# Later head sums and two multiplications on GpSimd in a decoder step, with the hand-overs between its stages rearranged

## The reference, cut to what matters

```python
u = rmsnorm(x, norm_mix) @ w_in               # q/k/v, r/k/v + low ranks, two gates of 1024 columns
us = u + mu_rw * (u_prev - u)                  # token shift
r, k, v, wl, al, gl = split(us)
decay = exp(-exp(-softplus(-(w0 + tanh(wl) @ w2)) - 0.5))
a = sigmoid(a0 + al @ a2);  g = sigmoid(gl) @ g2
kk = heads(k * k_k) / norm_of_head(k * k_k)    # a sum over each head's 64 features
k_mod = k * (1 + (a - 1) * k_a)
S, o = scan(S * d - (S kk)(kk * a)^T + v k^T)  # over tokens
bonus = sum_of_head(r * k_mod * r_k) * v       # the second sum over each head: "head sums"
mixed = (sig(gA) * (oa @ p_a) + sig(gB) * ((norm(o) + bonus) * g @ p_b)) @ w_o
```

## Time and profile before

| | |
|---|---|
| median of 3 runs | 1637.89 us |
| profiled execution: its own time | 1645.24 us |
| its span | 1643.5 us |
| PE busy | 1514.0 us (92%) |
| DVE busy | 680.5 us (41%) |
| POOL (GpSimd) busy | 497.4 us (30%) |
| ACT busy | 362.0 us (22%) |
| mean granted TensorE clock | 0.970 |

### The profile page before, as it was taken

How to read it: one execution, slowest core, us unless ns; L and a number is a source line. 1 busy time by engine, 2 the same in 40 slices (tenths; PEclk the granted TensorE clock), 3 DMA queues, 4 the chain that set the end, 5 groups by cost and what they waited for, 6 DMA issues and landing times. The chain is left out here.

```text
span 1643.5 us, 29192 instructions
## 1 busy us (share of the span) xinstructions
PE 1514.0 (92%) x12025; PEld 869.6 (53%) x12025; DVE 680.5 (41%) x1295; ACT 362.0 (22%) x711; POOL 497.4 (30%) x506
## 2 busy tenths in 40 slices
PE   7999998989999999999999999899999599999992
PEld 4664455455777787755667775444444233323320
DVE  4203144433268887651554333235384222222225
ACT  3002144454123332011211111112012111111122
POOL 3001055654323345415334320000227312222224
PEclk9999999999999999989999999899999799999996
DMA  6603298999531112454231214654401779999997
GB/s 232 231 35 115 80 325 321 374 354 347 173 134 59 58 66 82 114 153 112 71 71 49 60 43 159 238 218 141 192 39 52 288 275 412 402 397 398 403 335 248
DMA packets 111478, 322.88 MB, mean 196 GB/s; under 512 B 31576, under 2 KB 41240, under 8 KB 100688
## 3 DMA queue, kind: packets, MB, share of 16 engines
q1 hardware_dynamic: 83200, 246.45, 40.7%
q0 software_dynamic: 26848, 70.25, 13.1%
q10 hardware_dynamic: 1296, 4.29, 0.7%
HBM read 270.78 MB, written 58.02 MB: 200 GB/s over the span
## 5 line engine op out<-in xcount | busy, mean ns | idle before, releaser
L1718 PE MATMUL gate_p<-rows,gate_w 128*128 128x352 f32 x576 | 182.5, 473 | 0.0
L1718 PEld LDWEIGHTS gate_p<-rows,gate_w 128*128 128x128 f32 x576 | 109.7, 194 | 63.9 <-ACT u_rw L1868 5.1
L2616 PE MATMUL x_p<-wgu,rows 128*32 128x512 f32 (+1 forms) x640 | 124.7, 616 | 2.8 <-DMA wgu<-in_we_gu 1.4
L2616 PE MATMUL x_p<-late,rows 128*32 128x512 f32 (+1 forms) x640 | 122.6, 599 | 0.0
L1683 POOL DMA_DIRECT2D t_ring<-t_blocks x128 | 69.3, 549 | 121.0 <-DVE tt L1937 117.7
L462 POOL DMA_INDIRECT rows<-in_cache_kT,page_index x41 | 42.0, 1025 | 190.6 <-PE fox_b L518 102.4
L2593 POOL DMA_INDIRECT y<-obT,moe_ent x24 | 25.0, 1040 | 219.7 <-DVE obT L2643 204.1
L1312 PE MATMUL rw_pp<-rows,rw_w 128*128 128x264 f32 x384 | 88.9, 387 | 1.8 <-DVE u_rw L1452 1.8
L2634 ACT ACTIVATE rows<-h_p,vec 128x128 f32<-128x128 f32 x96 | 27.5, 369 | 246.1 <-PE h_p L2611 246.1
L1312 PEld LDWEIGHTS rw_pp<-rows,rw_w 128*128 128x128 f32 x384 | 72.5, 190 | 15.7 <-issue 3.6
L2643 DVE SCALAR_TENSOR_TENSOR obT<-x_p,moe_scales,late 128x1024 f32<-128x1024 f32 x24 | 30.8, 1284 | 115.0 <-PE x_p L2628 115.0
(11 more groups left out here) (532 smaller groups left out, 2872.0 us busy)
## 6 DMA issues: line engine op xcount, KB each, us to landing
wgu<-in_we_gu SPq DMA_DIRECT2D x16, 2048.0 KB, 12.5
late<-in_we_gu SPq DMA_DIRECT2D x16, 2048.0 KB, 10.0
wd<-in_we_down SPq DMA_DIRECT2D x16, 1024.0 KB, 8.7
late<-in_we_down SPq DMA_DIRECT2D x16, 1024.0 KB, 12.6
rows<-in_cache_kT SPq DMA_DIRECT2D x41, 256.0 KB, 5.2
y<-const SPq DMA_DIRECT2D x9, 1024.0 KB, 5.1
rows<-in_cache_v SPq DMA_DIRECT2D x34, 256.0 KB, 7.4
gate_rows<-u_rw SPq DMA_DIRECT2D x48, 176.0 KB, 1.8
```

The lines of the kernel that those rows point to most:

```text
L1718: mm = pe.matmul(out[:, 0:GATE_N], gw[:, j % 2, k, :], e.xnT[:, k, at], start=(k == 0), stop=(k == KD - 1))
L2616: mm = pe.matmul(gu[d][at:at + n, :], hT[:, d, k, at:at + n], wgu[u][:, k, :], start=(k == 0), stop=(k == KD - 1))
```

## The change

It does five things. (1) `at_b` is 23 + 10p, and for p of 1 and above the base of all other steps of a head pair, on PE, ACT and DVE, is one half product later; the first grams stand at t = 56 instead of 55. (2) For the first three head pairs beta times exp and alpha times exp run on GpSimd (`scale`) instead of DVE, at fixed places in its list, with the semaphore `scaled`. (3) The front's last gate store and the scan's last gate store and state store count on semaphores of their own and are waited for in the next stage; SP's other waits at the front's end stand ahead of the last pair's stores. (4) The scan's units begin with three gate units; the gains follow one column later. (5) `oaT` is loaded after the store of unit 15 instead of at the scan's start.

```diff
-    if _c < FRONT_GATES + 6:
-        UNITS.append(("gain", 2 * (_c - FRONT_GATES)))
+    if 0 < _c - FRONT_GATES <= 6:
+        UNITS.append(("gain", 2 * (_c - FRONT_GATES - 1)))
     UNITS.append(("gate", 3 * _c))
+    if 0 < _c - FRONT_GATES <= 6:
+        UNITS.append(("gain", 2 * (_c - FRONT_GATES) - 1))
     UNITS.extend([("gate", 3 * _c + 1), ("gate", 3 * _c + 2)])
+OA_AFTER = 15
...
-    at_z, at_a, at_s, at_b = ({t + 10 * p: p for p in range(HP)} for t in (13, 14, 16, 22))
-    at_grams = {55: 0, 59: 1}
+    at_z, at_a, at_s = ({t + 10 * p + (p > 0): p for p in range(HP)} for t in (13, 14, 16))
+    at_b = {23 + 10 * p: p for p in range(HP)}
+    at_grams = {56: 0, 59: 1}
...
-            store_gates(len(PAIRS) - 1)
             sp.wait_ge(last_kept, len(ORDER))
             sp.dma_start(a["shift_out"], last[:]).then_inc(stored, 16)
             sp.wait_ge(stored, 32)
             sp.wait_ge(y2_filled, 16 * NTT)
-            sp.wait_ge(gate_stored[0], 16 * (FRONT_GATES // 2))
-            sp.wait_ge(gate_stored[1], 32 * (FRONT_GATES // 2))
             sp.wait_ge(x_back, 16)
             sp.wait_ge(l_stored, 16 * 16)
+            store_gates(len(PAIRS) - 1)
+            sp.wait_ge(gate_stored[0], 16 * (FRONT_GATES // 2))
+            sp.wait_ge(gate_stored[1], 32 * (FRONT_GATES // 2) - 16)
...
+            def scale(p):
+                pool.wait_ge(exps, 2 * p + 1)
+                pool.wait_ge(cum_ready, p + 1)
+                pool.tensor_tensor(e.beta[:, p], e.beta[:, p], t2[:], ALU.mult).then_inc(scaled, 1)
+                pool.wait_ge(exps, 2 * p + 2)
+                pool.tensor_tensor(e.alpha[:, p], e.alpha[:, p], t1s[p % 2][:], ALU.mult).then_inc(scaled, 1)
...
             for q in range(len(PAIRS)):
                 weight_sums(q)
+                if q in (2, 5):
+                    scale((q - 2) // 3 * 2)
...
+                if q == 3:
+                    scale(1)
...
-                t1, base = t1s[p % 2], 10 * p
+                t1, base = t1s[p % 2], 10 * p + (p > 0)
...
-                dve.tensor_tensor(e.beta[:, p, m], e.beta[:, p, m], t2[:, m], ALU.mult)
+                if p == HP - 1:
+                    dve.tensor_tensor(e.beta[:, p, m], e.beta[:, p, m], t2[:, m], ALU.mult)
...
-                dve.tensor_tensor(e.alpha[:, p, m], e.alpha[:, p, m], t1[:, m], ALU.mult)
+                if p == HP - 1:
+                    dve.tensor_tensor(e.alpha[:, p, m], e.alpha[:, p, m], t1[:, m], ALU.mult)
...
-            sp.dma_start(e.oaT, e.oa_d).then_inc(oa_back, 16)
...
+                if n == OA_AFTER:
+                    sp.dma_start(e.oaT, e.oa_d).then_inc(oa_back, 16)
...
+                    if c == 0:
+                        act.wait_ge(e.front_tail, 16)
                     act.wait_ge(q["made_tok"], c + 1)
...
+            sp.wait_ge(e.scan_tail, 32)
             sp.dma_start(gain[:], e.gate_d[2 * KD:].rearrange("h p n -> p h n")).then_inc(gain_loaded, 16)
```

More of the change, by code:

```diff
@@ L44 @@
 for _c in range(FRONT_GATES, NCH):
-    if _c < FRONT_GATES + 6:
-        UNITS.append(("gain", 2 * (_c - FRONT_GATES)))
+    if 0 < _c - FRONT_GATES <= 6:
+        UNITS.append(("gain", 2 * (_c - FRONT_GATES - 1)))
     UNITS.append(("gate", 3 * _c))
-    if _c < FRONT_GATES + 6:
-        UNITS.append(("gain", 2 * (_c - FRONT_GATES) + 1))
+    if 0 < _c - FRONT_GATES <= 6:
+        UNITS.append(("gain", 2 * (_c - FRONT_GATES) - 1))
     UNITS.extend([("gate", 3 * _c + 1), ("gate", 3 * _c + 2)])
+OA_AFTER = 15
 UNIT_STEPS = list(accumulate({"gate": KD, "gain": 1}[_kind] for _kind, _ in UNITS))
@@ L169, in build @@
         e.w_first_loaded = ctx.enter_context(nc.semaphore("w_first_loaded"))
+        e.front_tail, e.scan_tail = ctx.enter_context(nc.semaphore("front_tail")), ctx.enter_context(nc.semaphore("scan_tail"))
         e.mix_first_loaded = ctx.enter_context(nc.semaphore("mix_first_loaded"))
@@ L1052, in stage_rwkv_front @@
                                                     sem("rw_rk"), sem("rw_made_b"), sem("rw_sum_kept"))
-    cum_ready, pair_done, t2_used = sem("rw_cum"), sem("rw_pair_done"), sem("rw_t2_used")
+    cum_ready, pair_done, t2_used, scaled = sem("rw_cum"), sem("rw_pair_done"), sem("rw_t2_used"), sem("rw_scaled")
     gate_stored, x_back = [sem(f"rw_gate_stored{x}") for x in range(2)], sem("rw_x_back")
@@ L1154, in store_gates @@
                 sp.wait_ge(combined, 4 * q + 4)
-                sp.dma_start(e.gate_d[2 * g + 1, :, 0:HN], t0[:, 0:HN]).then_inc(gate_stored[1], 16)
+                sp.dma_start(e.gate_d[2 * g + 1, :, 0:HN], t0[:, 0:HN]).then_inc(gate_stored[1] if q + 1 < len(PAIRS) else e.front_tail, 16)
             for q in range(1, len(PAIRS)):
@@ L1222, in _ @@
                     pool.wait_ge(pair_done, 3)
+                    pool.wait_ge(scaled, 2 * HP - 2)
                     pool.wait_ge(t_made, 4)
@@ L1248, in lower_grams @@
                 pe.wait_ge(pair_done, HP)
+                pe.wait_ge(scaled, 2 * HP - 2)
                 if g:
@@ L1392, in _ @@
                     act.wait_ge(pair_done, p - 1)
+                    act.wait_ge(scaled, 2 * (p - 1))
                 act.wait_ge(made_a, p + 1)
@@ L1400, in _ @@
                     act.wait_ge(pair_done, p)
+                    act.wait_ge(scaled, 2 * p - 1)
                 act.wait_ge(shifted, 3 + 2 * p)
@@ L1412, in _ @@
                 act.activation(t3[:], t3[:], ACT.Exp).then_inc(exps, 1)
-                keep_products(base + 22)
+                keep_products(23 + 10 * p)
                 act.wait_ge(made_b, p + 1)
@@ L1635, in _ @@
                     sp.wait_ge(q["state_ready"], NCH + 1)
-                    sp.dma_start(a["wkv_prompt"], state[:]).then_inc(stored, 16)
+                    sp.dma_start(a["wkv_prompt"], state[:]).then_inc(e.scan_tail, 16)
                 sp.wait_ge(q["unit_kept"], n + 1)
@@ L1641, in _ @@
                 row, r = (j if kind == "gate" else 2 * KD + j), n % GATE_RING
-                sp.dma_start(e.gate_d[row, :, third * GATE_N:(third + 1) * GATE_N], gate[:, r]).then_inc(gate_stored[r], 16)
+                sp.dma_start(e.gate_d[row, :, third * GATE_N:(third + 1) * GATE_N], gate[:, r]).then_inc(gate_stored[r] if n + 1 < len(UNITS) else e.scan_tail, 16)
+                if n == OA_AFTER:
+                    sp.dma_start(e.oaT, e.oa_d).then_inc(oa_back, 16)
                 if kind == "gate" and third == 2 and j + 2 < 2 * KD:
                     sp.dma_start(gw[:, j % 2], a["w_in"][24 + j]).then_inc(w_loaded[j % 2], 16)
-            sp.wait_ge(stored, 16)
             sp.wait_ge(oa_back, 16)
             for s in range(GATE_RING):
-                sp.wait_ge(gate_stored[s], 16 * ((len(UNITS) + GATE_RING - 1 - s) // GATE_RING))
+                sp.wait_ge(gate_stored[s], 16 * ((len(UNITS) - 1 + GATE_RING - 1 - s) // GATE_RING))
         @block.gpsimd
```

1 line of the change is left out of this document (removed).

## The result

The changed kernel takes 1648.96 us (median of 17 runs, 1644.72 to 1653.04) against 1642.4 us of the kernel before (median of 17 runs beside it, 1634.51 to 1651.0): the ratio is 1.004, 95% interval 1.0024 to 1.0055. It is 0.4% slower, some 6.6 us, where 1624 us was forecast.

What follows compares the result with a forecast made beforehand. PE was taken to set the front's pace, and PE to bound the rest of the scan. Terms: -2.4 front, -0.9 hand-over, -6.7, -3.0 first fill, -1.0 scan's end = -14.0 us, giving 1624 us; range 1613 to 1640.

Steps and rivals of the forecast that it cites:

- Pair 0: Front, first head pair: P2 keeps its date of 512.90 and the decay projection follows it, a loss of 2.0 us.
- Pair 1: Front: the 2.93 us wait goes to about nothing; 0.5 us ahead after P7 and the bonus sums.
- Pair 2: Front: its lag before was small; the new order is 1.1 us ahead after P4 and its bonus sums.
- Pair 3: Front: 2.6 of a 3.06 us wait stay; P7 with these sums 3.4 us ahead, the last product 2.4 earlier.
- The multiplications: Front: six moved to GpSimd, each freeing 1.25 us of DVE; DVE's slowing, 0 to 6 x 0.95 us, taken as 0.
- Rival E: Front: each multiplication on GpSimd stops DVE for 2.43 us, +7 on the chain instead of -2.4; 1633 us, chance 0.08.
- The hand-over: Front to scan: xn_rows' load starts when P5 is done; PE starts 3.3 us earlier, 0.9 of it from this.
- The first fill: Scan's start: first gate unit at 3.6 us, blocks at 9.5, across(0) at 57.8 without a wait: -6.7, half clock -3.0 us.
- Rival C: First fill: gate weights and their own small pieces slow the blocks, not oaT; ring stays at 64.5; 1634 us, chance 0.13.
- Rival D: First fill: the ring's slot is late and meets oaT, loads stretch by 9.9 us; slower, 1643.5 us, chance 0.10.
- Scan to mix: Scan's end: with the last store out of the way, -1.0 us (0 to 1.3); 1.6 us instead of 2.5.
- The base: Starting time of the forecast: the median of three runs, with the profiled execution of 1645.24 us 7.35 above it.

Runs made afterwards that it cites:

- e8: The kernel before with the later sums and grams alone, but pair 0's bonus sums at their old place (t = 22): 1646.31 us, ratio 1.0028.
- e9: The kernel before with the later sums alone, but the first grams at t = 55 again instead of 56: 1644.06 us, ratio 0.9995.
- e1: The changed kernel with parts 1 and 2 (later sums, multiplications on GpSimd) taken out: 1638.36 us, ratio 0.9965 to the kernel before.
- e5: e1 with SP issuing the last pair's stores right after shift_out, its waits behind them: 1636.74 us, ratio 0.9967 to the kernel before.
- e11: e5 with oaT loaded at the scan's start as before, the units' new order kept: 1642.93 us, ratio 0.9988 to the kernel before.
- e4: The changed kernel without the multiplications on GpSimd, which are on DVE again: 1645.07 us, ratio 1.0004 to the kernel before.
- e10: e5 with oaT loaded after the store of unit 3 instead of unit 15: 1634.71 us, ratio 0.9933 to the kernel before.
- e13: e10 with the front's second last store also awaited in the scan, later sums for pairs 1 to 3, grams at 55: 1634.83 us, ratio 0.9955 to before.
- e7: e2 with DVE's combine(base + 21) ahead of the bonus operand, for all head pairs: 1651.06 us, ratio 1.0049 to the kernel before.
- e2: The kernel before with part 1 alone (later sums, grams at 56), all multiplications on DVE: 1648.21 us, ratio 1.0023.

## Why the prediction was wrong

The forecast was 14.0 us of gain; it became 6.6 us of loss. The mechanism failed in the front, in three steps: what DVE and GpSimd take from each other was put at nothing, and so was the move of the grams, and SP's queue at the front's end was not looked at. The part on the scan was right. Where both orders have done the same products, in the two traces, the changed kernel stands against the one before:

| point | forecast | measured |
|---|---|---|
| pair 0 done | 2.0 behind | 2.9 behind |
| P7 and the sums of pair 1 | 0.5 ahead | 0.8 behind |
| P4 and the sums of pair 2 | 1.1 ahead | 2.9 behind |
| P7 of q = 6, sums of pair 3 done | 3.4 ahead | 2.1 behind |
| P3 of q = 6 and the first grams | not in the sum | 6.1 behind |
| last product | 2.4 ahead | 7.3 behind |
| scan's first product | 3.3 ahead | 9.3 behind |

By its own steps:

**Pair 0: right in kind, short by the clock.** The loss of 2.0 us at P2 was forecast, and e8 shows it by itself. Not foreseen was that P1 would wait at once for a combination which DVE does only behind L1526 (3.43 us) and run at half clock behind that wait, 1.7 us more. P6 of q = 2 starts 0.9 us later with a projection of 2.0 us still to do: 2.9 in place of 2.0.

**Pair 1: the wait went as forecast,** 2.93 to 0, and to at most 0.32 in the other runs with the later sums. Half product P5 behind it waits 0.75 us for ACT, where 0.4 was forecast.

**Pair 2: the first failed step.** I saw that L1520 took 2.21 us beside GpSimd's sums in pair 1 and 1.26 in pair 2, let the slow ones of pair 1 go, and did not ask whose instructions would now lie beside GpSimd. Those of pair 2 did. DVE and GpSimd in the changed kernel:
```profile
596.52 2.25 DVE L1538 TENSOR_TENSOR u_rw<-u_rw,rw_t 128x1056 f32<-128x1056 f32 x1
598.80 1.69 DVE L1539 TENSOR_SCALAR rw_t<-rw_t,vec 128x1056 f32<-128x1056 f32 x1
595.23 2.42 POOL L1245 TENSOR_TENSOR u_rw<-u_rw 128x528 f32<-128x528 f32 x1 [5.82 <-ACT u_rw L1393]
597.61 2.31 POOL L1246 TENSOR_TENSOR u_rw<-u_rw 128x528 f32<-128x528 f32 x1
```
GpSimd's two are the sums of result halves, 1.30 us each alone. The same DVE operations take 1.26 and 0.77 us in pair 1, with nothing beside them, so 1.9 us are lost, and the sums wait 1.65 us where they had not waited. What follows P4 and these sums starts at 605.14 instead of 602.24. Another 0.99 us of it is the multiplications' wait at 574.70.

**Pair 3 and the end: the step that was missing.** The part on pair 3 gained 0.8 us where 2.3 was forecast; its terms came true (the wait is 2.54, P6's wait for ACT is gone), but the multiplications' wait of 1.65 stood against them. It named no price for the grams at t = 56. They had stood between P5 and P3 and covered the combination that P3 waits for. This combination stands in DVE's list behind pair 3's last product. Without the cover P3 waited 2.18 us and took 5.49 instead of 3.83. That product of DVE was itself held up by GpSimd. In the changed kernel, then in the kernel before:
```profile
658.63 2.43 POOL L1224 TENSOR_TENSOR u_rw<-rows 128x1056 f32<-128x1056 f32 x1
658.70 3.48 DVE L1558 TENSOR_TENSOR u_rw<-u_rw,rw_t 128x1056 f32<-128x1056 f32 x1
```
```profile
651.55 1.25 DVE L1538 TENSOR_TENSOR u_rw<-u_rw,rw_t 128x1056 f32<-128x1056 f32 x1
653.92 2.42 POOL L1214 TENSOR_TENSOR u_rw<-rows 128x1056 f32<-128x1056 f32 x1
```
The new order puts GpSimd's token sums (`token_sum_again`) beside pair 3's last product, which takes 3.48 instead of 1.25 us. It takes 3.47 to 3.49 in every run with the later sums, also where the multiplications are on DVE. The 2.2 us are as long as P3's whole wait, and the 1.33 that the grams wait in e9 end with the same product. No run takes this overlap away, so how much of the wait would go with it is not shown. And as the grams came later against the end, so did their 16 block stores, which SP issues for 18 us, and the load of xn_rows behind them. e9 shows both by undoing this number alone.

**The multiplications: the cheap end was taken.** Rival E had the right mechanism at a chance of 0.08. The rows put DVE's loss at up to 2.3 us for one instruction, not the 0.95 that I bounded it with. The Trainium skill ("SBUF — State Buffer", Who interferes with whom) says that a DVE instruction with two SBUF inputs and a GpSimd instruction reading SBUF block each other for the whole instruction, and that copies can too when they run in the mode that uses both ports. The trace agrees, at 3.48 instead of 1.25 us for a product and 2.41 instead of 0.16 for the 16-column copy. Rival E's "+7 on the chain" was too much for the end, though: some of the lost time fell into DVE's idle stretches, and the waits came to 2.6 us.

**The hand-over: a queue not looked at.** "The load starts when P5 is done" held no longer, for P5 was done some 7 us before the end and the load went out 5.4 before it, behind the block stores. It landed after 7.0 us, at 704.2; the store of shift_out, issued behind it at 699.21 and counted with its old 1.9 us, took 5.1 and landed at 704.3, and the last pair's stores came only then. 0.9 us of gain became 2.0 of loss. In e1, with the old front and the load out in time, the order alone gave 0.3 (3.25 against 3.59). With the waits behind the stores (e5) the gap is 2.0 us.

**The first fill: right, nearly to the number.** First gate unit at 4.4 us (forecast 3.6, which e1 has), blocks at 10.7 (9.5), `across(0)` at 57.9 (57.8) without a wait and at full clock. The time from the scan's first product to the next tokens fell from 72.9 (771.75 - 698.87) to 63.5 us (771.70 - 708.18), 9.4 against 6.7 + 3.0 forecast. Rival C is out by e11.

**Rival D was there in small.** `oaT` did meet the ring, but its second slot: 1.5 us of wait, 1.0 of issue and a half-clock stretch. I had called this the tightest point and looked only at the first slot.

**Scan to mix:** 2.50 to 1.26 us, forecast 1.6.

The base was wrong as well: the kernel before is at 1641 to 1646 in all the comparisons, not at 1637.9, so even a gain of 14 would have come to about 1628.

## What to carry to other kernels

- When a small step is moved away from ahead of a waiting instruction, ask for every place that it left what it covered there. One number in a list of places cost more than all the planned waits gave back, because the step had hidden a combination and, through a queue, the last load of the stage.
- Where an engine's chain sets a date, moving waits on the other engine ahead of that date changes their names and not their sum. Count both sides from one date to the next before any order is changed.
- An overlap that slows a chain does not vanish when the order shifts by a slot. It lands on another instruction: look which. Here a slow stretch left pair 1 and came up in pair 2, and pair 3's last product, never slow before, took 3.48 instead of 1.25 us.

## What the runs showed of the hardware that was not expected

- A DVE copy of 16 columns took 2.41 instead of 0.16 us beside a GpSimd product of 128x1056, and that product 3.45 instead of 2.43 us. A short instruction paid the whole rest of the other engine's long one. In pair 1 DVE's scan over 128x1056 took 4.47 instead of 2.36 us beside the multiplications.
- Four loads of 128 KB land in 12.6 to 14.3 us (median) beside a 2112 KB load and in 5.8 to 6.5 without it.
- A store of 63 KB landed in 5.1 to 5.7 us where it was issued right behind a load of 1056 KB (changed kernel, e1, e4, e5, e10 to e13) and in 1.9 where it went out 7.6 us behind it (before, e9).
- Waits of like length were followed by half clock in some profiles and not in others: 2.36 us by a product of 5.49 (e8), 3.23 and 2.20 by products of 3.80 (e7, e13), and P1 of q = 2 took 6.79, 6.49, 5.49 and 5.46 us after the same wait of 3.4 (e2, e4, e9, changed kernel). In the changed kernel's runs the mean clock went from 0.976 to 0.967 and the time from 1645.0 to 1652.6 us with it. One trace of each kernel can hide a difference of 0.4%.
